# Attention stages of a two-part transformer kernel: biased score and row maximum in one VectorE instruction, scaling of the probabilities on GpSimd, results copied out by VectorE

## What is computed

```
def mla_attend(q_n, q_r, k_n, k_r, v):
    s = jnp.einsum('bqhd,bkhd->bhqk', q_n, k_n) + jnp.einsum('bqhr,bkr->bhqk', q_r, k_r)
    p = jax.nn.softmax(s.astype(jnp.float32) * MLA_SCALE, axis=-1).astype(v.dtype)
    out = jnp.einsum('bhqk,bkhd->bqhd', p, v)
```

## Time and profile before

| | us |
|---|---|
| three runs | 4495.84, 4501.09, 4506.28 (median 4501.09) |
| span of the profiled execution | 4503.0 |
| mla stage, first scores to last copy | 65.7 |
| attn stage, first layer | 85.1 |
| attn stage, second layer | 85.2 |
| the three together | 236.0 (5.2% of the span) |
| VectorE busy in the three | 206.9 |
| TensorE busy in the three | 211.0 |
| GpSimd busy in the three | 6.3 |

### The profile page before, as it was taken

The page is one execution under the profiler, slowest core; times in us unless marked ns, Lnnn a source line. Parts: engine busy times, 40 slices in busy tenths (PEclk is TensorE's granted clock), DMA queues, the critical chain, the costliest instruction groups (busy, mean ns, idle before and its releaser), DMA issues. The chain is left out here.

```text
span 4503.0 us, 74169 instructions
## 1 busy us (share of the span) xinstructions
PE 4053.7 (90%) x28216; PEld 3863.1 (86%) x28216; DVE 3288.5 (73%) x5810; ACT 2040.8 (45%) x3498; POOL 1164.3 (26%) x1015
## 2 busy tenths in 40 slices
PE   7887988999999996659999999799898989989898
PEld 4676988999999995549999999699688989978897
DVE  6885898778788885567987788666576676657666
ACT  5243335667333333224444455444564454446444
POOL 0000003667788870100169454100000000000000
PEclk9998999999999998879999999899899999989999
DMA  6332446998999993325876788554234545422453
GB/s 248 108 127 95 143 156 199 339 320 288 321 333 330 335 321 131 110 84 191 263 237 208 270 296 299 167 186 161 84 110 155 185 151 189 162 101 93 150 189 124
DMA packets 281606, 896.15 MB, mean 199 GB/s; under 512 B 29424, under 2 KB 73424, under 8 KB 278822
## 3 DMA queue, kind: packets, MB, share of 16 engines
q1 hardware_dynamic: 223286, 673.80, 44.0%
q0 software_dynamic: 55520, 201.60, 13.2%
q10 hardware_dynamic: 2448, 16.02, 0.9%
HBM read 834.92 MB, written 56.14 MB: 198 GB/s over the span
## 5 line engine op out<-in xcount | busy, mean ns | idle before, releaser
L153 DVE TENSOR_TENSOR weight_lo<-weight_ring,weight_hi 128x1024 fp32r<-128x1024 f32 x1084 | 1356.6, 1252 | 709.1 <-ACT weight_hi L148 695.2
L148 ACT ACTIVATE weight_hi<-weight_ring 128x1024 fp32r<-128x1024 f32 x1084 | 1142.9, 1054 | 1304.5 <-issue 741.3
L185 PE MATMUL pair0e_acc<-pair_xh,weight_hi 128*128 128x384 f32 (+1 forms) x1152 | 409.8, 356 | 10.5 <-ACT pair0e_gelu L2521 8.5
L185 PE MATMUL pair0e_acc<-pair_xl,weight_hi 128*128 128x384 f32 (+1 forms) x1152 | 398.7, 346 | 0.0
L185 PE MATMUL pair0e_acc<-pair_xh,weight_lo 128*128 128x384 f32 (+1 forms) x1152 | 398.3, 346 | 0.0
L185 PE MATMUL pair0e_acc<-pair0e_coef_hi,weight_hi 128*128 128x384 f32 x1024 | 343.1, 335 | 7.9 <-DVE pair0e_coef_lo L2235 7.9
L185 PE MATMUL pair0e_acc<-pair0e_coef_lo,weight_hi 128*128 128x384 f32 x1024 | 342.7, 335 | 0.0
L185 PE MATMUL pair0e_acc<-pair0e_coef_hi,weight_lo 128*128 128x384 f32 x1024 | 342.6, 335 | 0.0
L185 PE MATMUL peer10e_dot<-peer_xh,weight_hi 128*128 128x224 f32 (+1 forms) x1152 | 324.2, 281 | 8.8 <-DVE weight_lo L153 5.7
L185 PE MATMUL peer10e_dot<-peer_xl,weight_hi 128*128 128x224 f32 (+1 forms) x1152 | 316.9, 275 | 0.0
L185 PE MATMUL peer10e_dot<-peer_xh,weight_lo 128*128 128x224 f32 (+1 forms) x1152 | 316.8, 275 | 0.0
(11 more groups left out here) (628 smaller groups left out, 12383.9 us busy)
## 6 DMA issues: line engine op xcount, KB each, us to landing
weight_ring<-in_w_tiles SPq DMA_DIRECT2D x572, 512.0 KB, 3.3
weight_ring<-in_peer_tiles SPq DMA_DIRECT2D x512, 512.0 KB, 4.6
pair_acts<-pair0e_gelu SPq DMA_DIRECT2D x64, 384.0 KB, 5.7
pair0e_act_in<-pair_acts SPq DMA_DIRECT2D x64, 384.0 KB, 5.2
peer_acts<-peer10e_gelu SPq DMA_DIRECT2D x64, 224.0 KB, 4.2
peer10e_act_in<-peer_acts SPq DMA_DIRECT2D x64, 224.0 KB, 4.9
pair_coefs<-pair0e_G ACTq DMA_DIRECT2D x12, 1024.0 KB, 15.0
pair0e_kept_in<-pair_coefs SPq DMA_DIRECT2D x64, 192.0 KB, 6.5
```

Of the source, the lines that this page charges most:

```text
L148: act.activation(self.tile_of(self.hi, g), self.ring[:, g % RING, :], ACT.Copy).then_inc(self.hi_done, 2)
L153: dve.tensor_tensor(self.tile_of(self.lo, g), self.ring[:, g % RING, :], self.tile_of(self.hi, g).bitcast(F32), ALU.subtract).then_inc(sel ...
L185: last = pe.matmul(out, lhsT, rhs, start=start and i == 0, stop=stop and i == len(passes) - 1, **more)
```

## The change

- VectorE's two passes of a batch with bias become one instruction per unit, a tensor_tensor_reduce that writes `biased` and the row maximum. It computes (raw + bias) × scale, so that the bias planes are kept eight times as large (the scale is 1/8 in attn); ScalarE multiplies by 8 in the copy that it makes anyway. Without bias nothing changes here.
- The multiplication of `prob` goes from VectorE to GpSimd, instruction for instruction. VectorE no longer waits for its own reciprocal, but signals it (`inverted`).
- Copying the results out goes from ScalarE to VectorE, at the end of a step, for batch s−2.
- In a step TensorE does the values of batch s−2 before the transposes of batch s−1.
- The row tiles of mla are issued by SyncE, not by GpSimd.

```
+        if side is not None:
+            @block.sync
+            def _(sync):
+                side.load(sync)
+
+        @block.gpsimd
+        def _(pool):
+            for s in range(steps):
+                pool.wait_ge(inverted, s + 1)
+                for u, i, x in batch(s):
+                    p, by = prob[:, s % 2, i, 0:x.nk], inverse[:, s % 2, i:i + 1]
+                    if x.weight is None:
+                        ins = pool.tensor_scalar(p, p, by, None, ALU.mult)
+                    else:
+                        ins = pool.tensor_scalar(p, p, by, x.weight, ALU.mult, ALU.mult)
+                    ins.then_inc(normed, 1)
...
-            for s in range(steps + 1):
+            for s in range(steps + 2):
...
                         if x.bias is not None:
-                            last = dve.scalar_tensor_tensor(out=biased[:, b, i, 0:x.nk], in0=raw[:, b, place(i), 0:x.nk],
-                                                            scalar=x.scale, in1=x.bias, op0=ALU.mult, op1=ALU.add)
-                    if now[0][2].bias is not None:
-                        chain(last)
-                    for u, i, x in now:
-                        src = raw[:, b, place(i), 0:x.nk] if x.bias is None else biased[:, b, i, 0:x.nk]
-                        last = dve.tensor_reduce(low[:, b, i:i + 1], src, X_AXIS, ALU.max)
+                            last = dve.tensor_tensor_reduce(biased[:, b, i, 0:x.nk], raw[:, b, place(i), 0:x.nk], x.bias,
+                                                            x.scale, NEG, ALU.add, ALU.max, low[:, b, i:i + 1])
+                        else:
+                            last = dve.tensor_reduce(low[:, b, i:i + 1], raw[:, b, place(i), 0:x.nk], X_AXIS, ALU.max)
                     chain(last)
...
-                    chain(dve.reciprocal(inverse[:, b, :], total[:, b, :]))
-                    for u, i, x in before:
...
-                        ins.then_inc(normed, 1)
+                    dve.reciprocal(inverse[:, b, :], total[:, b, :]).then_inc(inverted, 1)
                 if side is not None:
-                    side.dots(dve, s + 1, steps + 1)
+                    side.dots(dve, min(s + 1, steps + 1), steps + 1)
+                for u, i, x in batch(s - 2):
+                    if x.end:
+                        dve.wait_ge(summed, u + 1)
+                        lo, hi, dst = x.out
+                        dve.tensor_copy(dst, out[lo:hi, group[u] % 2, 0:P]).then_inc(evacuated, 1)
...
-                for u, i, x in batch(s - 2):
-                    if x.end:
-                        act.wait_ge(summed, u + 1)
-                        lo, hi, dst = x.out
-                        act.activation(dst, out[lo:hi, group[u] % 2, 0:P], ACT.Copy).then_inc(evacuated, 1)
...
-                act.activation(bias[:, 2 * n:2 * n + 2, :], acc[:, n % 4, :, :], ACT.Copy).then_inc(copied, 1)
+                act.activation(bias[:, 2 * n:2 * n + 2, :], acc[:, n % 4, :, :], ACT.Copy, scale=8.0).then_inc(copied, 1)
```

More of the change, by code:

```diff
@@ L1058, in attention @@
         low, total, inverse, sunk = (S.sb(n, [P, 2, B]) for n in ("low", "total", "inverse", "sunk"))
-        scored, shifted, exped, normed, transposed, copied, summed, evacuated, v_ordered, a_ordered = (
-            S.sem(n) for n in ("scored", "shifted", "exped", "normed", "transposed", "copied", "summed",
+        scored, shifted, exped, inverted, normed, transposed, copied, summed, evacuated, v_ordered, a_ordered = (
+            S.sem(n) for n in ("scored", "shifted", "exped", "inverted", "normed", "transposed", "copied", "summed",
                                "evacuated", "v_ordered", "a_ordered"))
@@ L1066, in attention @@
         if side is not None:
-            @block.gpsimd
-            def _(pool):
-                side.load(pool)
+            @block.sync
[12 more added lines that the diff above has]
+                    ins.then_inc(normed, 1)
         @block.tensor
@@ L1083, in _ @@
                 scores(s + 1)
-                for u, i, x in batch(s - 1):
-                    pe.wait_ge(normed, u + 1)
-                    if i % H == 0 and s >= 2:
-                        pe.wait_ge(copied, u - B + H)
-                    for b in range(x.nk // P):
-                        last = pe.transpose(turned[:, i, b * P:(b + 1) * P], prob[:, (s - 1) % 2, i, b * P:(b + 1) * P], ident)
-                    last.then_inc(transposed, 1)
                 for u, i, x in batch(s - 2):
@@ L1099, in _ @@
                     last.then_inc(summed, 1)
+                for u, i, x in batch(s - 1):
+                    pe.wait_ge(normed, u + 1)
+                    if i % H == 0 and s >= 2:
+                        pe.wait_ge(copied, u - B + H)
+                    for b in range(x.nk // P):
+                        last = pe.transpose(turned[:, i, b * P:(b + 1) * P], prob[:, (s - 1) % 2, i, b * P:(b + 1) * P], ident)
+                    last.then_inc(transposed, 1)
         @block.vector
@@ L1134, in _ @@
                         chain(dve.tensor_tensor(total[:, b, :], total[:, b, :], sunk[:, b, :], ALU.add))
-                    chain(dve.reciprocal(inverse[:, b, :], total[:, b, :]))
-                    for u, i, x in before:
-                        p, by = prob[:, b, i, 0:x.nk], inverse[:, b, i:i + 1]
-                        if x.weight is None:
-                            ins = dve.tensor_scalar(p, p, by, None, ALU.mult)
-                        else:
-                            ins = dve.tensor_scalar(p, p, by, x.weight, ALU.mult, ALU.mult)
-                        ins.then_inc(normed, 1)
-                if side is not None:
-                    side.dots(dve, s + 1, steps + 1)
+                    dve.reciprocal(inverse[:, b, :], total[:, b, :]).then_inc(inverted, 1)
+                if side is not None:
+                    side.dots(dve, min(s + 1, steps + 1), steps + 1)
[4 more added lines that the diff above has]
+                        dve.tensor_copy(dst, out[lo:hi, group[u] % 2, 0:P]).then_inc(evacuated, 1)
             if side is not None:
```

## The result

The changed kernel takes 4523.87 us in the median of six runs (4512.71 to 4543.63), the kernel before 4501.91 (4495.84 to 4508.16). The ratio is 1.0051, with a 95% interval of 1.0033 to 1.0069: slower by 15 to 31 us. I had forecast 4497.5, which is within 0.2% of no change, with 4519 as the upper end of the range. The profiled execution of the changed kernel was its fastest, 4512.71 us with a span of 4510.9, against the 4503.0 of the other trace.

The account below looks back on a forecast made before the run. VectorE was taken to set attn's pace, with TensorE just as full in mla at 512 keys. Two attn layers at −3.5 us each and mla +3.5 took the span from 4503.0 to 4499.5, forecast median 4497.5 us, range 4471 to 4519.

Parts of the forecast that it names:

- GpSimd's price: GpSimd's multiplication: 0.70 and 0.90 us for 128 and 256 columns with two factors; 0.50, 0.70, and 1.10 at 512, with one.
- Rival 2: Scaling in every loop round: GpSimd as dear as the 0.79 us row, growing with columns, total 4516 us; chance 0.25.
- N: GpSimd's four multiplications in an attn round: 3.07 us in a sparse-branch step, 2.8 in a differential, 2.4 in a sink step.
- The sum of mla: mla: 512 keys 4.74 us a step, +3.0 us; 256 keys 3.4 against 3.33, +0.5; end unchanged; +3.5 us in all.
- while the loop fills: First steps run before the round through in-order lists closes: 2 us off in mla, 1.5 us off in each attn.
- The end stays: End of mla: unchanged, about 4.5 us after the last reciprocal.
- The sum of attn: Each attn layer: pace 3.98 against 3.88 us, +1.8; start −1.5, first steps −1.5, end −2.3; −3.5 us a layer.
- my sum of 4.66: Sparse-branch round in attn, two steps: hand-overs, scores, values, copy, combined instructions, shift and reciprocal, 4.66 us, plus N.
- rival 1: GpSimd is cheap and TensorE sets the pace, attn 3.29 us a step: total 4468, halfway 4476 at pace 3.47; chance 0.27.
- The loop: In-order lists: VectorE's copy waits for values ahead of the next maxima, one round per two steps; wait near 1.5 us a step.
- rival 3: The loop is absent, copies rarely making VectorE wait; attn pace is GpSimd's own load, 3.1 us, total 4469; chance 0.06.
- Free edits: Scale of 8 in ScalarE's existing copy, and mla's twelve tile issues moved to SyncE: both cost nothing.

## Why the prediction was wrong, point by point

The step that failed is a term of the sums that was mis-sized, the price of GpSimd's one-factor multiplication. With the two-factor form in its place the stages changed by +3.8 us in mla and by −5.0 and −4.1 in attn, where I had forecast +3.5, −3.5 and −3.5, and the ratio, 0.9985, is near the forecast 0.9992. In part that is luck, as the points below show: the single terms were off both ways.

**What bounded the kernel: right.** VectorE set the pace of attn; relieving it of 0.9 us a step and nothing else brought 8.8 us a stage.

**The combined instruction: right.** Its rows in the changed kernel read 272 to 425 ns, 0.28 and 0.41 as said. The start of attn was forecast 1.5 us shorter, and it was: 5.02 us to the first reciprocal against 6.54.

**GpSimd's price: the step that failed.** "With one factor 0.50 and 0.70, and 1.10 at 512 columns" measured 0.60, 0.92 and 1.56, and 2.46 for a unit of 512 beside a dot product; two factors were to cost 0.70 and 0.90 and cost 0.45 and 0.56. I took it for granted that one factor cannot be dearer than two, and no row of the kernel before showed the one-factor form. Rival 2 had 0.6 and 0.9 for it, by luck, but charged them to the sparse-branch steps, where N fell to 1.9 us and not above 3.65. The price decided in the sink steps (N = 3.05, not 2.4), and most of all in mla. The experiments put the one-factor form at 12 us in mla and 5.6 in attn of layer one: without it the change is a little faster than the kernel before, 0.9985.

**The sum of mla: wrong by 12 us.** +3.5 forecast, +15.9 measured. The charge for the dot products, 1.1 us a round, was near the measured 0.9; the pair of units itself costs 3.1 us, not 2.2. In the closed round this did not show much: from the third reciprocal to the eighth a step takes 4.91 us (forecast 4.74). It shows at the start. I took 2 us off "while the loop fills", but the very first round is closed already: the third reciprocal stands in VectorE's list behind the copies of the first batch, and these wait for its values. From the first reciprocal to the third it takes 14.0 us where my sum leaves 7.5. Of the 6.5 us, 2.0 are what I took off, 1.8 are the first two units, which take 5.05 us (226.94 to 231.99, both beside dot products) where I had 3.3, and 2.5 are the low clock behind TensorE's waits for them, which my sum has no term for. The seven steps from the eighth on took 3.74 us each, not 3.4 (2.4 us). "The end stays" missed 2.6 us.

**The sum of attn: −3.5 forecast, +0.6 in this trace.** From the first to the nineteenth reciprocal and to the end:

```profile
3243.29 0.18 DVE L1144 RECIPROCAL attn_inverse<-attn_total 128x4 f32<-128x4 f32 x1 [0.62 <-ACT attn_prob L1167]
...
3314.89 0.18 DVE L1144 RECIPROCAL attn_inverse<-attn_total 128x4 f32<-128x4 f32 x1
...
3323.47 0.29 DVE L1151 COPY second_y<-attn_out 64x128 f32<-64x128 f32 x1 [0.38 <-PE attn_out L1102]
...
3315.16 5.95 POOL L1078 TENSOR_SCALAR attn_prob<-attn_prob,attn_inverse 128x128 f32<-128x128 f32 x8 [2.32 <-DVE attn_inverse L1144]
```

The difference of 4.1 us lies in two terms: the 1.5 us that I took off while the loop fills did not come, and the end grew by 0.4 us instead of falling by 2.3. The pace is 71.60/18 = 3.98 us, the very number of the forecast, but by luck: N, GpSimd's four units of a step, was 1.1 us shorter in a sparse-branch step, and a term was missing. With the measured prices my formula gives 3.68. Two sparse-branch rounds of the changed kernel show that term. First the rows of one round, then those of the next:

```profile
3264.32 0.17 DVE L1144 RECIPROCAL attn_inverse<-attn_total 128x4 f32<-128x4 f32 x1
...
3266.11 0.44 POOL L1080 TENSOR_SCALAR attn_prob<-attn_prob,attn_inverse,second_gates 128x128 f32<-128x128 f32 x1
...
3266.86 1.13 PE L1089 MATMUL attn_raw<-second_heads 64*128 64x256 f32 x4
...
3269.56 0.28 DVE L1151 COPY second_y<-attn_out 64x128 f32<-64x128 f32 x1 [2.91 <-PE attn_out L1102]
...
3271.06 0.17 DVE L1144 RECIPROCAL attn_inverse<-attn_total 128x4 f32<-128x4 f32 x1
...
3266.49 0.17 DVE L1144 RECIPROCAL attn_inverse<-attn_total 128x4 f32<-128x4 f32 x1
...
3267.61 1.10 POOL L1080 TENSOR_SCALAR attn_prob<-attn_prob,attn_inverse,second_gates 128x256 f32<-128x256 f32 x2
3269.81 0.82 PE L1110 MATMUL attn_turned<-const_sb,attn_prob 128*128 128x128 f32 x6
...
3275.20 0.17 DVE L1144 RECIPROCAL attn_inverse<-attn_total 128x4 f32<-128x4 f32 x1
```

The first round takes 6.74 us for two steps, where my sum of 4.66 with N = 1.96 gives 6.62. Its parts are within 0.5 us of mine, some longer and some shorter. The second takes 8.71. GpSimd is done at 3268.71, but the transposes start at 3269.81, since TensorE's list has the scores and values of the other batch ahead of them. Two rounds share TensorE; each lets it go for some 3.3 us, and the other's part is 3.4 to 3.7 us long. I had treated a round as if it had TensorE to itself. One of my signs says the same: TensorE was to wait 0.5 to 1 us a step for GpSimd, and its products waited 3.9 and 3.3 us in all in the two stages, under 0.2 a step (its weight loads, which run ahead of them, 0.5 in layer one), since it had the other round's work to do. The same term is missing in rival 1: with cheap GpSimd work everywhere attn's pace was 67.34/18 = 3.74, not the 3.47 that I gave for it. At the end, forecast to fall from 8.5 to 6.2 us, the two sink batches' 5.95 us of GpSimd kept it at 8.9. And in other executions low clock comes on top, 2 us a stage in the mean.

**The loop: right, and larger than I said.** VectorE waits 74.1 us for values in front of its copies in both attn stages, 1.85 us a step (forecast 1.5), so rival 3 is out. But GpSimd's scaling alone showed that a round through the scores exists without any copy on VectorE.

**Free edits: right.** Nothing in the changed trace waits for a tile of mla in VectorE's list.

**What stays open:** why the clock falls after the gap in one execution and not in another, and how often in the changed kernel itself. That two interleaved rounds share TensorE is read from one trace and agrees with the pace of another (3.74); no kernel was built to take that share away alone.

## What to carry to other kernels

Work that is moved off a full engine pays with its latency wherever in-order lists close a round that sets the pace (here 2 us a stage in one order of TensorE's list, nothing in the other): write the round down, with every engine's share in it, and count two interleaved rounds on the engine they share. Price each form of an instruction by a row of that very form; here leaving an operand out cost 1.6 to 2.3 times as much, and writing a 1.0 in its place took that away. Try the parts of a bundle one by one: one part alone was worth 20 us, and the others ate it.

## What the runs showed of the hardware that I had not expected

- GpSimd's multiplication by one per-row factor takes 604, 923 and 1563 ns at 128, 256 and 512 columns of float32; with a second factor, the constant 1.0, it takes near 370, 475 and 690, and with a second per-row factor 450 and 558 at 128 and 256.
- A unit of 512 columns that starts beside a 1024-column dot product of VectorE takes 0.9 us more, 2.46 instead of 1.56 with one factor and 1.59 instead of 0.69 with two.
- After a stretch in which TensorE was busy 6.78 of 8 us its granted clock was 0.52 and 0.50 for the next 16 us in one execution, and 1.00 in another with the same instructions and the same gap. In mla it fell to 0.50 for 6.8 us in the second of two waits of 1.8 and 1.9 us.
